# Head norms of block 1 placed in front of attention, and norm factors from ScalarE's root with one Newton step

## The reference, cut to what matters

```python
def rmsnorm(x, g):
    xf = x.astype(jnp.float32)
    y = xf * lax.rsqrt(jnp.mean(xf * xf, axis=-1, keepdims=True) + EPS)
    return (y * g.astype(jnp.float32)).astype(x.dtype)

# block 1, one layer (the second block: same norms, gates in the place of gains)
    h = rmsnorm(x, attn_norm[l])
    c_q, c_kv, k_r, q_d, k_d, v_d = jnp.split(h @ w_in[l], split_at, axis=-1)
    q = (rmsnorm(c_q, g_cq) @ w_uq).reshape(B, S, MLA_HEADS, MLA_QK)
    kv = (rmsnorm(c_kv, g_ckv) @ w_ukv).reshape(B, S, MLA_HEADS, MLA_NOPE + MLA_V)
    q = rmsnorm(q, g_qn)          # per head of 96; then rope, dense attention
    k = rmsnorm(k, g_kn)
    q_d = rmsnorm(q_d.reshape(B, S, DIL_HEADS, DIL_HD), g_dil_q[l])   # per head of 64; dilated attention
# block 2, ends of its stages
    x = x + ga1 * rmsnorm_2(mix_x, g_post_mix[i])
    x = x + ga2 * rmsnorm_2(yx, g_post_ffn[i])
```

## Time and profile before

| | |
|---|---|
| time, median of 3 runs | 1913.75 us (1913.57 to 1914.12) |
| the profiled execution's own time | 1916.09 us |
| its span | 1914.0 us |
| TensorE busy | 1710.8 us (89%) |
| VectorE busy | 1143.2 us (60%) |
| ScalarE busy | 769.8 us (40%) |
| granted TensorE clock, mean | 0.944 |

### The profile page before, as it was taken

How to read it: one execution, slowest core, us unless ns; L and a number is a source line. 1 busy time by engine, 2 the same in 40 slices (tenths; PEclk the granted TensorE clock), 3 DMA queues, 4 the chain that set the end, 5 groups by cost and what they waited for, 6 DMA issues and landing times. The chain is left out here.

```text
span 1914.0 us, 25429 instructions
## 1 busy us (share of the span) xinstructions
PE 1710.8 (89%) x9822; PEld 1427.6 (75%) x9822; DVE 1143.2 (60%) x2209; ACT 769.8 (40%) x1248; POOL 255.3 (13%) x310
## 2 busy tenths in 40 slices
PE   6979899989798999889799789999999596979996
PEld 6657899876568998678557568888787484669985
DVE  5585676455857775543774754444333746577754
ACT  4443555344434554422143333333212432545542
POOL 2000011700011117100000001111630000001161
PEclk9989999999898999889989899999999798989998
DMA  7344666555459554422064323333222242126651
GB/s 218 122 167 154 177 178 190 184 158 162 144 160 263 146 164 177 154 66 72 22 219 156 109 69 92 107 89 109 82 95 89 88 125 57 45 79 186 178 183 58
DMA packets 265341, 253.21 MB, mean 132 GB/s; under 512 B 8681, under 2 KB 208589, under 8 KB 265222
## 3 DMA queue, kind: packets, MB, share of 16 engines
q1 hardware_dynamic: 262111, 244.66, 41.6%
q0 software_dynamic: 2464, 6.67, 1.1%
q10 hardware_dynamic: 647, 0.26, 0.1%
HBM read 250.49 MB, written 1.06 MB: 131 GB/s over the span
## 5 line engine op out<-in xcount | busy, mean ns | idle before, releaser
L1115 DVE TENSOR_TENSOR wL<-ring,wH 128x1024 fp32r<-128x1024 f32 (+2 forms) x364 | 453.4, 1251 | 331.2 <-ACT wH L1637 328.3
L1637 ACT ACTIVATE wH<-ring 128x1024 fp32r<-128x1024 f32 (+2 forms) x364 | 376.3, 1040 | 340.7 <-PE psv L538 329.5
L538 PE MATMUL psv<-hH,wH 128*128 128x256 f32 (+1 forms) x1504 | 471.4, 313 | 4.5 <-issue 4.5
L538 PE MATMUL psv<-hL,wH 128*128 128x256 f32 (+1 forms) x1504 | 469.6, 312 | 0.0
L538 PE MATMUL psv<-hH,wL 128*128 128x256 f32 (+1 forms) x1504 | 469.5, 312 | 0.0
L538 PEld LDWEIGHTS psv<-hH,wH 128*128 128x128 f32 x1504 | 288.6, 192 | 24.8 <-issue 9.4
L538 PEld LDWEIGHTS psv<-hL,wH 128*128 128x128 f32 x1504 | 288.7, 192 | 15.7
L538 PEld LDWEIGHTS psv<-hH,wL 128*128 128x128 f32 x1504 | 288.7, 192 | 15.7
L965 POOL TENSOR_TENSOR W<-scr 128x256 f32<-128x256 f32 (+1 forms) x88 | 77.5, 880 | 1343.2 <-ACT scr L1731 1343.2
L1726 ACT ACTIVATE scr<-psv,colp 128x256 f32<-128x256 f32 (+1 forms) x176 | 109.0, 619 | 340.9 <-PE psv L538 340.6
L1223 DVE SCALAR_TENSOR_TENSOR scr<-psv,colp,scr 128x255 f32<-128x255 f32 (+1 forms) x176 | 96.5, 548 | 201.9 <-ACT scr L1726 201.7
(11 more groups left out here) (221 smaller groups left out, 2030.9 us busy)
## 6 DMA issues: line engine op xcount, KB each, us to landing
ring<-in_w_up SPq DMA_DIRECT2D x176, 512.0 KB, 5.2
ring<-in_w_mod SPq DMA_DIRECT2D x96, 512.0 KB, 4.7
ring<-in_w_down SPq DMA_DIRECT2D x88, 512.0 KB, 4.2
ring<-in_w_in SPq DMA_DIRECT2D x52, 512.0 KB, 4.7
ring<-in_w_out SPq DMA_DIRECT2D x32, 512.0 KB, 4.6
ring<-in_w_in SPq DMA_DIRECT2D x8, 384.0 KB, 4.1
ring<-in_w_in SPq DMA_DIRECT2D x8, 288.0 KB, 5.4
ring<-in_w_ukv SPq DMA_DIRECT2D x4, 512.0 KB, 4.6
```

Source lines behind the costliest of these rows:

```text
L538: return pe.matmul(o, a, b, start=start, stop=stop, skip_group_check=True)
L1115: v.tensor_tensor(lo, raw, hi.bitcast(F32), ALU.subtract).then_inc(piece_split, told("piece_split", p))
L1637: return ac.activation(o, i, ACT.Copy)
```

## The change

Four things are edited. (1) `rms` is replaced by `inverse`: four VectorE instructions, a reciprocal of a root and one Newton step. (2) ScalarE makes that root: behind each sum of squares stand two more activations, `Sqrt` and `Identity`, that write the root and the mean; behind each head reduction `head_root` does four (two for the context keys), for which VectorE first hands over its sums (`head_sums`) and later waits (`head_roots`). (3) All lift banks are read by ScalarE (`kinds="SS"`, so TensorE writes them to the PSUM banks of ScalarE). (4) In block 1 the MLA heads' sum, norm and rotation stand in front of "in 4" and `dT` on VectorE, with the squares in two halves on ScalarE.

```diff
@@ vector
-            def rms(dst, sums, n, scale=None):
...
+            def inverse(dst, x, roots):
+                v.reciprocal(dst, roots).then_inc(vector_step, step())
                 v.wait_ge(vector_step, steps[0])
+                v.tensor_tensor(t, dst, dst, ALU.mult).then_inc(vector_step, step())
                 v.wait_ge(vector_step, steps[0])
+                v.scalar_tensor_tensor(t, t, -0.5, x, ALU.mult, ALU.mult).then_inc(vector_step, step())
                 v.wait_ge(vector_step, steps[0])
+                v.scalar_tensor_tensor(dst, t, 1.5, dst, ALU.add, ALU.mult).then_inc(vector_step, step())
                 v.wait_ge(vector_step, steps[0])
...
-                        v.wait_ge(sum_of_squares, at("sum_of_squares", ph, t))
-                        rms(rr[:, t:t + 1], ss[:, t:t + 1], D)
+                        v.wait_ge(root_ready, at("root_ready", ph, t))
+                        inverse(rr[:, t:t + 1], ss[:, t:t + 1], root[:, t:t + 1])
...
+                v.wait_ge(head_roots, at("head_roots", ph, "dil"))
+                inverse(hr[:, 0:32], hx[:, 0:32], hroot[:, 0:32])
...
+                for t in range(NT):
+                    v.wait_ge(head_squares, at("head_squares", ph, "mla", t))
+                    v.tensor_reduce(hx[:, 32 + 16 * t:48 + 16 * t], sqm[t], AX_X, ALU.add).then_inc(head_sums, told("head_sums", ph, "mla", t))
...
+                splits_to(first_piece[ph, "in", 4], 2)
+                v.wait_ge(head_roots, at("head_roots", ph, "mla"))
+                inverse(hr[:, 32:64], hx[:, 32:64], hroot[:, 32:64])
+                splits_to(first_piece[ph, "in", 4] + 3, 0)
...
                 rotate(x1, x2, tab, tmp).then_inc(mla_heads, told("mla_heads", ph))
+                input_rows(4, dvh[:, 0, :, :])
+                for t in range(NT):
+                    v.wait_ge(V_full, at("V_full", ph, "dT", t, 0))
...
@@ tensor
-                        project(latT[:, base:base + kin, :], w, n, range(NT), (ph, "lift", base, c), c0=n * c if base else 0)
+                        project(latT[:, base:base + kin, :], w, n, range(NT), (ph, "lift", base, c), c0=n * c if base else 0, kinds="SS")
@@ scalar
                 ac.activation(junk[:, 0:n], x, ACT.Square, accum_out=ss[:, c:c + 1]).then_inc(sum_of_squares, mark("sum_of_squares", *key))
+                ac.wait_ge(sum_of_squares, at("sum_of_squares", *key))
+                ac.activation(root[:, c:c + 1], ss[:, c:c + 1], ACT.Sqrt, scale=1.0 / n, bias=eps_col[:, 0:1])
+                ac.activation(ss[:, c:c + 1], ss[:, c:c + 1], ACT.Identity, scale=1.0 / n, bias=eps_col[:, 0:1]).then_inc(root_ready, mark("root_ready", *key))
...
+            def head_root(h_, x, n, cq, *key):
+                e = (HD, MQK).index(n) + 1
+                for f, o in ((ACT.Sqrt, h_), (ACT.Identity, x)):
+                    if cq:
+                        ac.activation(o[:, :, 0:cq], x[:, :, 0:cq], f, scale=1.0, bias=eps_col[:, e:e + 1])
+                    ins = ac.activation(o[:, :, cq:], x[:, :, cq:], f, scale=1.0 / n, bias=eps_col[:, 0:1])
+                ins.then_inc(head_roots, mark("head_roots", *key))
...
+                ac.wait_ge(dil_heads, at("dil_heads", ph))
+                for t in range(NT):
+                    ac.wait_ge(V_free, at("V_free", ph, "in", 1, 0))
+                    ac.wait_ge(S_free, at("S_free", ph, "lift", 3, 1, t))
+                    ac.activation(sqm[t], qk[:, t, :, :], ACT.Square).then_inc(head_squares, mark("head_squares", ph, "mla", t))
...
@@ scalar, block 2, behind the squares of the heads and ahead of the Fourier banks
+                ac.wait_ge(head_sums, at("head_sums", ph, 0))
+                if last:
+                    ac.wait_ge(head_sums, at("head_sums", ph, 2))
+                    head_root(h_[:, 2:4, 8:10], x[:, 2:4, 8:10], HD, 0, ph, "context")
+                head_root(h_[:, 0:nt, :], x[:, 0:nt, :], HD, 8, ph)
```

More of the change, by code:

```diff
@@ L131, in build @@
         hr = sb("hr", [P, 64])
-        nwt = sb("nwt", [P, 2, 64])
+        hx = sb("hx", [P, 64])
+        eps_col = sb("eps_col", [P, 4])
+        root = sb("root", [P, 16])
+        hroot = sb("hroot", [P, 64])
+        nwt = sb("nwt", [P, 64])
         posi = sb("posi", [P, 2], mybir.dt.int32)
@@ L994, in _ @@
             gp.memset(ones33[:, :], 1.0).then_inc(ones_written, mark("ones_written", "all"))
+            for i, n in enumerate((1, HD, MQK)):
+                gp.memset(eps_col[:, i:i + 1], n * EPS).then_inc(ones_written, mark("ones_written", "all"))
             gp.memset(csil[:, :, :], 0.0).then_inc(ones_written, mark("ones_written", "all"))
@@ L1078, in wrap @@
                 return v.tensor_scalar(r, r, PI_IN, -PI_IN, ALU.min, ALU.max)
-            def rms(dst, sums, n, scale=None):
-                v.wait_ge(newest[0], newest[1])
+            def inverse(dst, x, roots):
+                t = nwt[:, 0:size(dst)]
+                if len(dst.shape) == 3:
+                    t = t.rearrange("p (t h) -> p t h", h=dst.shape[2])
+                v.reciprocal(dst, roots).then_inc(vector_step, step())
                 v.wait_ge(vector_step, steps[0])
[L1084 to L1087, removed]
+                v.tensor_tensor(t, dst, dst, ALU.mult).then_inc(vector_step, step())
                 v.wait_ge(vector_step, steps[0])
-                v.tensor_scalar(t.bitcast(I32), x.bitcast(I32), 1, None, ALU.logical_shift_right).then_inc(vector_step, step())
+                v.scalar_tensor_tensor(t, t, -0.5, x, ALU.mult, ALU.mult).then_inc(vector_step, step())
                 v.wait_ge(vector_step, steps[0])
-                v.tensor_scalar(y.bitcast(I32), t.bitcast(I32), -1.0, 1597463007.0, ALU.mult, ALU.add).then_inc(vector_step, step())
+                v.scalar_tensor_tensor(dst, t, 1.5, dst, ALU.add, ALU.mult).then_inc(vector_step, step())
                 v.wait_ge(vector_step, steps[0])
[L1094 to L1103, removed]
             split_n = [0]
@@ L1372, in _ @@
                 splits_to(first_piece[ph, "in", 2])
-                v.wait_ge(sum_of_squares, at("sum_of_squares", ph, "lat", 3, 1))
-                v.tensor_scalar(ss[:, 8:10], ss[:, 8:10], float(KVL / QL), None, ALU.mult).then_inc(vector_step, step())
-                v.wait_ge(vector_step, steps[0])
-                rms(rr[:, 8:12], ss[:, 8:12], KVL)
+                v.wait_ge(root_ready, at("root_ready", ph, "lat", 3, 1))
+                inverse(rr[:, 8:12], ss[:, 8:12], root[:, 8:12])
                 for base, off, n in ((0, 0, QL), (3, QL, KVL)):
@@ L1390, in _ @@
                 v.wait_ge(head_squares, at("head_squares", ph, "dil"))
[L1391 to L1394 removed]
+                v.tensor_reduce(hx[:, 0:32].rearrange("p (k h) -> p k h", k=8), sqd.rearrange("p k (h d) -> p k h d", h=4),
+                                    AX_X, ALU.add).then_inc(head_sums, told("head_sums", ph, "dil"))
@@ L1417, in _ @@
-                v.wait_ge(head_squares, at("head_squares", ph, "mla"))
-                v.wait_ge(newest[0], newest[1])
-                v.wait_ge(vector_step, steps[0])
-                v.tensor_reduce(hr[:, 32:64], sq_heads.rearrange("p (h d) -> p h d", h=32), AX_X, ALU.add).then_inc(vector_step, step())
-                v.wait_ge(vector_step, steps[0])
-                head_scale(hr[:, 32:64], MQK)
                 v.wait_ge(sine_done, at("sine_done", "rope"))
@@ L1791, in _ @@
                         copy(toep[:, h, :], bank("S", "band", h)[:, 0:TOEP]).then_inc(S_free, mark("S_free", "band", h))
-                ac.wait_ge(V_free, at("V_free", ph, "lift", 3, 1, 0))
-                ac.wait_ge(S_free, at("S_free", ph, "lift", 3, 1, 1))
-                ac.activation(sq_heads, qk[:, :, :, :].rearrange("p t h d -> p (t h d)"), ACT.Square).then_inc(head_squares, mark("head_squares", ph, "mla"))
+                ac.wait_ge(head_sums, at("head_sums", ph, "mla", 1))
+                head_root(*(a[:, 32:64].rearrange("p (t h) -> p t h", t=NT) for a in (hroot, hx)), MQK, 8, ph, "mla")
                 input_rows(4, dvh[:, 1, :, :])
```

83 lines of the change are left out of this document (34 added, 49 removed).

## The result

The changed kernel takes 1858.39 us in the median of 4 runs (1857.46 to 1859.44), the kernel before in the same comparison 1913.66 us. The ratio is 0.9712 with a 95% interval of 0.9695 to 0.9729. The profiled execution's own time is 1857.46 us, its span 1855.6.

What follows compares the result with a forecast made beforehand. The prediction took VectorE's list at stage boundaries, where TensorE stands still, as the bound. Its terms summed to -39.2 us, from the median 1913.75 to 1874.6, say 1875 us (forecast 1866 to 1886; range 1860 to 1895).

Steps and rivals of the forecast that it cites:

- Rival C: Whole kernel: shorter gaps keep TensorE's clock up, some 12 us more gain, 1863 us; chance 0.12.
- The clock's test in the prediction: Whole kernel: a mean TensorE clock over 0.955 would show that the clock gains too and the forecast is wrong.
- The idle terms: Stages of both blocks: changes in TensorE's waiting, summed to -39.2 us.
- the feed-forward of block 1 layer 1: Two-tile boundary in block 1: +0.25 us, since it ends behind a transfer anyway.
- the first mix of block 2: Start of block 2: four shorter norms, less a table load and longer chains, -3.2 us.
- Attention: Block 1: first scores come earlier as MLA head work moves ahead; -8.2 us in layer 0, -3.6 in layer 1.
- rival A: Block 1 attention: moved MLA work gains nothing, late low parts starve "in 4" by over 6 us; 1886 us, chance 0.12.
- Heads of block 2: Layer 0: Fourier banks start 4.4 us late behind head roots, a gap of 3.38 absorbs most; +1.8 us.
- Who is the bound: Stage boundaries: VectorE's list is the bound; over four tiles each norm saves 1.54 us, less one load at the front.
- D's sign: Norms: VectorE always waits over 1.5 us for ScalarE's root, ScalarE being the bound; 1940 or 1926 us, chance 0.04.
- The price of the pair: Each norm's two added ScalarE activations: 0.32 us each, lengthening ScalarE's list by 0.42 us.
- Table loads: ScalarE, before a stage's first root: ten more at 1.28 us each, nine on a stage's first chain.

Runs made afterwards that it cites:

- e13: The changed kernel with the extra throw-away products of e12 and none of its other edits: 6.1 us faster than the changed kernel.
- e12: e11 with more throw-away products cut to TensorE's remaining gaps: another 11.8 us faster than e11.
- e11: The changed kernel with early throw-away Sqrt at eight stages, head roots behind first Fourier banks, reordered "in 4" and a later filter network: 1847.65 us.
- e6: The changed kernel without its throw-away products at boundaries (110 of 0.44 us): 12.7 us slower than the changed kernel.
- e5: The kernel before with throw-away products cut to TensorE's gaps, norms and order untouched: 5.3 us faster than the kernel before.
- e9: The changed kernel with two throw-away root activations added ahead of each of 42 roots of row sums: 19.1 us slower than the changed kernel.
- e1: The kernel before with only the new order (lifts read by ScalarE, MLA head work ahead of "in 4") and twelve-step norms: 12.5 us faster.
- e10: The changed kernel with block 2's filter network two column steps later: 1.5 us slower than the changed kernel, within noise.
- e4: The changed kernel with a throw-away Sqrt ahead of the wait at nine stages, to load tables early: 1.2 us faster, not told from the changed kernel.

## Why the prediction was wrong

The direction was right, and so was what the sum counted; one part of the gain was left out of it: -55.3 for -39.2.

- **The step that failed** is the treatment of TensorE's clock. Rival C had it, as a case beside the sum with a chance of 0.12 and 12 us. It belonged in the sum: each of my terms shortened a gap, and the real products, the same in both kernels, took 20.3 us less in the profiles. Between median executions the time at 1.2 GHz fell by some 71 us. A us of it costs 0.23 us of the time within one kernel; between kernels, by median times and median clocks, 0.19 (e13), 0.27 (e12 against e11), 0.16 (e6) and 0.09 (e5, where the filler itself may stand in the way). For 71 us that is 6 to 19, and 16 by the 0.23, which is what was missing. The clock's test in the prediction, a mean over 0.955, was met by all four executions (0.962 to 0.969).
- **The idle terms** held as a sum, 37 for 39. Two terms missed by some 3 us in idle time: at the feed-forward of block 1 layer 1 it rose by 3.4 and not 0.25, and at the first mix of block 2 it fell by 0.5 and not 3.2. Their stages still came out at +0.25 and -4.1. That the stage sums look so good is in part luck: the clock covered such misses. As e9 shows, idle time and slow work pass into each other, so only their sum is a test of a term.
- **Attention**: layer 0 gained 8.2 as walked; layer 1 5.3 for 3.6, with "in 4" waiting 3.26 us, under the 6 that rival A needed. A falls by e1.
- **Heads of block 2**: the late banks came (5.04 - 0.69 = 4.35 us for 4.4) and the gap of 3.38 behind them shrank to 0.35, as forecast. TensorE stood 3.1 us longer in that stage, which still gained 1.3 instead of losing 1.8, with 10.3 us less at 1.2 GHz.
- **Who is the bound.** I took VectorE to be still the bound over four tiles, and it is: 14 of 20 norms there start without a wait for the root (under 0.04 us). D's sign, waits at all norms, is not there. The price of the pair was right (0.29 and 0.28 us for 0.32 each, 0.4 in a row). The new norm takes 0.77 us on VectorE (1051.64 to 1052.41), as the sum had it, though the prediction's own items, 3 x 0.193 + 0.157, make 0.74.
- **Table loads**: 1.28 us each with no drain. For the Trainium skill (ScalarE: Activation LUTs, section "What ACT_TABLE_LOAD costs") a switch is 2.66 us; the rows above do not agree, and no term was changed for it.

## What to carry over

Where the bounding engine stands at stage boundaries, count the time it then works at the lower clock in the same term as the gap: here each us of gap that went gave about 1.5 us. Fill the gaps that remain with throw-away products of just their length, measured in time on the trace and not in records, and look at the clock behind each, since in e5 one such block changed nothing. Moving small serial steps from one engine to another pays where the receiver has a pause in front of them; after it, double the moved piece, as e9 did, and read the waits and not only the time, since the time also holds the clock. Before two profiles are compared, look whether the profiled executions are typical of their kernels.

## What was not expected of the hardware

TensorE with 55 us less work was 12.7 us slower (e6). Stretches at 1.2 GHz differ between kernels at places where instructions and idle time are alike (10.2 us against 3.4 in e10), so kernels that are 2 to 4 us apart may differ by this as much as by the edit: runs of e4 spread over 7.7 us, of e5 over 12.4, those of the changed kernel over 2.0.
